# Experts' stage of a two-model kernel: router and token rows taken from unnormalised tiles, expert numbers planned first, last sums inside the loop, output in four pieces

## The chip, the cores and the metric

One Trainium2 chip, one core. The time is device microseconds of one execution; the kernel before has three timed runs. All data and weights are 32-bit floats.

## The reference

The input is 256 tokens of width 1024. A first network of four layers runs, then a second of two layers, whose last part is what the change touches:

```python
h = rmsnorm_2(x, norm_ffn[1])             # x * rsqrt(mean(x*x) + 1e-5) * w
logits = (hf @ w_router)                  # 256 x 8
top_vals, top_idx = lax.top_k(logits, 2)
gates = jax.nn.softmax(top_vals, axis=-1)
# each token goes through its two experts:
expert(xb, e) = (silu(xb @ w_gate[e]) * (xb @ w_up[e])) @ w_down[e]   # 1024 -> 3584 -> 1024
x = x + sum over the two experts of gate * expert(h)
return rmsnorm_2(x, norm_final)
```

The norm divides a whole token by one number, its root mean square, so it changes neither which two logits are largest nor their order. It scales the difference of the two, on which the gates depend.

## The kernel before, in words

The residual stream X lies transposed in SBUF, as eight tiles of 128 channels x 256 tokens. The program is written out by hand for five queues that meet at semaphores: PE (matmuls), DVE, ACT, POOL and SP, which issues the weight loads. The order of work on each is the order of the code; nothing schedules it.

**Into the experts.** `residual` on DVE adds the last product of the second mixer to X two tiles at a time (L1599) and squares them (L1549, summed into S by L1557). `norm` then makes the normalised tiles H: PE sums the squares over channels (`summed`, L600, two records of the profile per call, as for all matmuls here), ACT takes the root (L1177), DVE inverts it and lays it on a diagonal (L1671, L1544), PE spreads it over the partitions (`spread_roots`, L608), and DVE multiplies eight tiles (L1680, H<-X). In other stages, those for which `early` holds, `residual` also writes U = X times the norm's gain (`u_tiles`, L1576), and PE's first product starts from U. `moe` was not one of them.

**Planning.** In `moe` PE multiplies H with the router's weights (L996, 128x8 results), then transposes H into token rows (L1001), which ACT copies to SBUF as `h_tok` (L1472). DVE picks the two best experts of each token (L2181 to L2196, `chosen`). Five small products of PE (L1007 to L1011) give each token's place within its expert and each expert's size. DVE computes the gates, ranks the experts by size, reorders seven facts by rank (L2228, L2232, `passes`), among them the expert's number, and writes the numbers as integers (`plan_i`, L2234). For those SP waits: it reads a number per expert and starts loading that expert's weights, slots of 2 MB into four buffers, a fifth for the last slot (L431). DVE then makes a placement matrix (`put`, L2240), and PE gathers the first expert's tokens with it from `h_tok` (`gather`, L1025), which ACT copies out in two halves (L1479).

**The expert passes.** Seven passes are written out, for experts in falling order of size with 4, 3, 3, 3, 3, 3 and 2 units of 32 tokens, and a loop follows with 2 units for the eighth expert and for tokens that did not fit. The number of loop passes comes from the data. A pass has 14 slots of up and gate weights (PE L1078) and 7 of down weights (L1104). After it ACT copies the result into `y_slot` (L1509), eight pieces for two units, and raises `y_done` once. `scatter` on PE (L1057) multiplies it back to the tokens' columns in four pieces of two tiles, and DVE adds each to X (`add`, L2298). In passes 1 to 6 the scatter of the pass before runs inside the next; that of the last static pass and of the loop passes stands at their end.

**The end.** After the loop DVE squares all of X (L1549), PE sums (L600), root, diagonal and spread follow as above, DVE writes eight tiles H (L1680), and SP stores H with one DMA of 1 MB (L442).

## Time and profile before

| | |
|---|---|
| median of 3 runs | 3094.98 us (3093.48 to 3096.37) |
| the profiled execution | 3095.92 us, its span 3094.1 us |
| PE busy | 2975.9 us (96%) |
| DVE, ACT busy | 1011.7 us (33%), 441.5 us (14%) |
| mean DMA rate | 243 GB/s |
| granted TensorE clock, mean | 0.989 of 2.4 GHz |

A row of the timeline gives start, duration, engine, line, operation and how many instructions it merges, and in brackets how long the engine was idle before and for whom it waited.

### The profile page before, as it was taken

The page shows a single profiled execution, that of the slowest core. Times are in us where ns is not written, and L with a number is a line of the kernel's source. Part 1 is how long each engine was busy: PE and PEld are TensorE (multiplying, and loading weights), DVE is VectorE, ACT ScalarE, POOL GpSimd, SP SyncE. Part 2 cuts the span into 40 slices and gives each one's busy share as a digit, 9 for nine tenths or more (in the row PEclk, how much of TensorE's full clock was granted, in tenths as well). Part 3 has the DMA queues.
Part 4 walks back from the last instruction along what each step waited for, and adds up shares of the span by engine and source line. Part 5 has one row for each costly group of instructions (what it writes and reads, how often), then busy time and mean ns, then how long its engine had stood idle before and what let it go on. Part 6 is the DMA issues. An engine that isn't in the chain of part 4 may idle for free.

```text
span 3094.1 us, 49146 instructions
## 1 busy us (share of the span) xinstructions
PE 2975.9 (96%) x21346; PEld 2233.0 (72%) x21346; DVE 1011.7 (33%) x2300; ACT 441.5 (14%) x902; POOL 92.9 (3%) x180
## 2 busy tenths in 40 slices
PE   5999997999999999999999999998999999999877
PEld 4888886888898888888888888885445345344334
DVE  5526633465354652223327400363100100100101
ACT  1102203221133210102202000121000100100100
POOL 1111000110001100000000000000000000000000
PEclk9999999999999999999999999998999999999998
DMA  9649642685434965444353444434789999999996
GB/s 374 262 176 361 225 162 82 242 319 174 163 109 167 351 214 179 144 142 150 137 166 121 136 151 142 158 108 198 292 321 389 367 382 392 365 382 392 425 421 264
DMA packets 96396, 750.56 MB, mean 243 GB/s; under 512 B 10576, under 2 KB 10960, under 8 KB 46032
## 3 DMA queue, kind: packets, MB, share of 16 engines
q1 hardware_dynamic: 70864, 655.48, 55.8%
q0 software_dynamic: 25344, 92.29, 8.1%
q8 instruction: 153, 2.51, 0.3%
q14 instruction: 35, 0.29, 0.0%
HBM read 746.68 MB, written 1.05 MB: 242 GB/s over the span
## 4 chain that ended last, share of the span: by engine, by line
PE 91%; DMA 5%; DVE 2%; ACT 1%; SPq 1%; issue 0%; DVEq 0%; ACTq 0%
PE ps L487 27%; PE ps L1078 17%; PE ps L564 16%; PE ps L1104 8%; PE ps L652 4%; PE ps L860 3%; PE ps L517 2%; PE ps L497 2%; PE ps L583 2%; PE ps L985 2%; PE ps L783 2%; DMA A<-w_moe_down 1%; PE ps L1057 1%; DMA B<-w_moe_down 1%; DMA B<-w_moe_up 1%; PE ps L1025 1%
## 5 line engine op out<-in xcount | busy, mean ns | idle before, releaser
L487 PE MATMUL ps<-H,ring 128*128 128x256 f32 x3872 | 838.5, 379 | 0.0
L487 PEld LDWEIGHTS ps<-H,ring 128*128 128x128 f32 x3872 | 735.1, 190 | 100.5 <-issue 1.0
L564 PE MATMUL ps<-A,ring 128*128 128x256 f32 x2272 | 491.5, 379 | 0.0
L564 PEld LDWEIGHTS ps<-A,ring 128*128 128x128 f32 x2272 | 431.7, 190 | 58.7
L1078 PE MATMUL ps<-ring,B 128*32 128x512 f32 (+1 forms) x3680 | 325.1, 509 | 11.5 <-DMA ring<-w_moe_up 11.2
L1078 PEld LDWEIGHTS ps<-ring,B 128*32 128x32 f32 x3680 | 121.8, 110 | 209.6 <-issue 157.7
L1078 PE MATMUL ps<-B 128*32 128x512 f32 x2208 | 242.3, 593 | 6.0 <-DMA B<-w_moe_up 6.0
L1800 DVE SCALAR_TENSOR_TENSOR C<-ps,vec,C 128x255 f32<-128x255 f32 (+1 forms) x336 | 146.5, 477 | 202.3 <-ACT C L1242 199.3
L2286 DVE TENSOR_TENSOR C<-C,ps 128x256 f32<-128x256 f32 (+1 forms) x92 | 35.7, 388 | 480.0 <-ACT C L1499 480.0
L1078 PEld LDWEIGHTS ps<-B 128*32 128x32 f32 x2208 | 71.7, 110 | 166.2 <-issue 155.3
L1708 DVE SCALAR_TENSOR_TENSOR B<-B,cact 128x1024 f32<-128x1024 f32 x160 | 188.8, 1220 | 8.6 <-DMA B<-w_ada 8.4
L1104 PE MATMUL ps<-B,A 128*32 128x256 f32 x2944 | 162.7, 379 | 9.5 <-DMA B<-w_moe_down 9.5
L1104 PEld LDWEIGHTS ps<-B,A 128*32 128x32 f32 x2944 | 94.9, 110 | 75.2 <-DMA B<-w_moe_down 13.4
L2298 DVE TENSOR_TENSOR X<-X,ps 128x512 f32<-128x512 f32 x32 | 22.0, 688 | 373.3 <-PE ps L1057 372.7
L860 PE MATMUL ps<-H,ring 128*128 128x256 f32 x640 | 143.8, 380 | 0.0
L1595 DVE SCALAR_TENSOR_TENSOR X<-ps,gcol,X 128x256 f32<-128x256 f32 x64 | 28.7, 480 | 333.1 <-PE ps L564 295.6
L860 PEld LDWEIGHTS ps<-H,ring 128*128 128x128 f32 x640 | 120.2, 190 | 16.8 <-issue 1.2
L1242 ACT ACTIVATE C<-ps,vec 128x256 f32<-128x256 f32 x168 | 85.7, 560 | 292.4 <-PE ps L487 289.8
L652 PE MATMUL ps<-ring,H 128*128 128x256 f32 x512 | 110.8, 379 | 0.0
L652 PEld LDWEIGHTS ps<-ring,H 128*128 128x128 f32 x512 | 97.3, 190 | 13.2
L462 POOL DMA_DIRECT2D B<-w_ada x144 | 75.7, 528 | 901.5 <-PE ps L583 516.3
L1499 ACT ACTIVATE C<-ps 128x256 f32<-128x256 f32 (+1 forms) x92 | 32.9, 358 | 468.9 <-PE ps L1078 468.9
(377 smaller groups left out, 2269.7 us busy)
## 6 DMA issues: line engine op xcount, KB each, us to landing
ring<-w_moe_up SPq DMA_DIRECT2D x64, 2048.0 KB, 10.2
B<-w_moe_up SPq DMA_DIRECT2D x48, 2048.0 KB, 10.3
ring<-w_ff_up SPq DMA_DIRECT2D x88, 1024.0 KB, 8.1
B<-w_ada POOLq DMA_DIRECT2D x144, 512.0 KB, 8.8
B<-w_moe_down SPq DMA_DIRECT2D x32, 2048.0 KB, 10.0
ring<-w_ff_down SPq DMA_DIRECT2D x64, 704.0 KB, 4.0
ring<-w_gm_in SPq DMA_DIRECT2D x32, 1024.0 KB, 5.0
ring<-w_moe_down SPq DMA_DIRECT2D x16, 2048.0 KB, 9.9
```

The lines of the kernel that those rows point to most:

```text
L462: pool.dma_start(buf, ins["w_ada"][ADA_FIRST + q]).then_inc(ready, 16)
L487: last = mm(bank[:, j * n:(j + 1) * n], ring[:, slot, k * 256 + j * P:k * 256 + j * P + P], src[:, k, :], start=(k == 0), stop=(k == KD - 1))
L497: last = mm(bank[:, j * TOK:(j + 1) * TOK], ring[:, slot, k * 256 + j * P:k * 256 + j * P + P], H[:, k, :], start=(k == 0), stop=(k == KD ...
L517: last = mm(bank[:, 0:n], ring[:, g0 % RING, o:o + P], U[:, k, 0:n], start=(k == 0), stop=(k == KD - 1))
L564: last = mm(bank, ring[:, g % RING, k * P:(k + 1) * P], src[:, kk, :], start=(kk == 0), stop=(kk == kt - 1))
L652: last = mm(ps[m % 4][:, t * TOK:(t + 1) * TOK], H[:, k, t * P:(t + 1) * P], ring[:, (g0 + m) % RING, k * 256:(k + 1) * 256], start=(k == ...
L860: last = mm(ps[t % 4][:, j * TOK:(j + 1) * TOK], ring[:, (g0 + t) % RING, o:o + P], H[:, k, :], start=(k == 0), stop=(k == KD - 1))
L1078: last = mm(ps[u][g * UNIT:(g + 1) * UNIT, 0:width], hg[:, k, u * UNIT:(u + 1) * UNIT], slot[:, (4 * i + g) * width:(4 * i + g + 1) * widt ...
L1104: last = mm(ps[4 + u // 2][g * UNIT:(g + 1) * UNIT, (u % 2) * TOK:(u % 2 + 1) * TOK], hidden_t(f, u), slot[:, i * D + g * TOK:i * D + (g + ...
L1242: ins = af(C[:, b % 4, half, :], src[:, half * TOK:(half + 1) * TOK], ACT.Identity, bias=vec[:, bass.ds(c + 3, 1)], scale=vec[:, bass.ds(c ...
L1708: return stt(out=w, in0=w, scalar=1.0, in1=cact[:, :], op0=ALU.mult, op1=ALU.mult, accum_out=mod[:, n:n + 1])
L1800: ins = stt(out=o, in0=src[:, half * TOK:(half + 1) * TOK - d], scalar=vec[:, c + 2 - d:c + 3 - d], in1=o, op0=ALU.mult, op1=ALU.add)
```

## The change

1. **U instead of H.** `residual` now calls `u_tiles` for `moe` too, and for the last tile before the square instead of after it. PE's `moe` starts with the router on U (six tiles, then the seventh, then the eighth, as they come), then the sums of squares, into ps[5]. `norm` of `moe` makes no diagonal, no spread and no H. The token rows are transposed from U, the first token half before the counting products and the second behind them, and ACT multiplies by the inverse root (one number per partition there) as it copies them. The difference of the two best logits is multiplied by the same number on DVE.
2. **Numbers first.** PE makes the sizes before the places. DVE ranks and writes `plan_i` from the one fact that it needs, then the four facts that `put` needs, then `put`; the gates, their exponential on ACT and the two gate facts come behind it.
3. **First expert.** Slots 0 and 1 of the first pass wait for the first half of the gathered tokens only, slot 2 for the second.
4. **Results out by piece.** ACT copies `y_slot` column group by column group and raises `y_done` four times a pass, and each piece of `scatter` waits for its own group.
5. **Last sums in the loop.** In every loop pass DVE squares two tiles of X right after each of the four adds, and PE sums pair m - 1 behind piece m of the scatter; the last pair is summed behind the loop. The squares behind the loop go.
6. **Output** in four DMAs of two tiles each.

```diff
-            h_ready.wait(sp, h_total)
-            sp.dma_start(out, H[:, :, :]).then_inc(out_done, 16)
-            sp.wait_ge(out_done, 16)
+            h_ready.wait(sp, h_total - KD)
+            for m in range(4):
+                h_ready.wait(sp, 2)
+                sp.dma_start(out[:, 2 * m:2 * m + 2, :], H[:, 2 * m:2 * m + 2, :]).then_inc(out_done, 16)
+            sp.wait_ge(out_done, 64)
...
+            def last_sums(m):
+
+                for k in (2 * m, 2 * m + 1):
+                    for t in range(2):
+                        last = mm(ps[5][:, t:t + 1], U[:, k, t * P:(t + 1) * P], mean[:, 0:1],
+                                  start=k + t == 0, stop=k == KD - 1 and t == 1)
+                return last
...
+                if kind == "final_2":
+                    pe.wait_ge(last_squared, ends[0] * 4)
+                    last_sums(3).then_inc(stat_done.sem, 1)
...
             def moe(_):
-                h_ready.wait(pe, KD)
+                for k in range(KD):
+                    if k in (0, 6, 7):
+                        u_ready.wait(pe)
+                    for t in range(2):
+                        last = mm(ps[4][:, t * 8:(t + 1) * 8], U[:, k, t * P:(t + 1) * P],
+                                  V("router", k * EXPERTS, EXPERTS), start=(k + t == 0), stop=(k == KD - 1 and t == 1))
+                last.then_inc(pe_done.sem, 1)
                 banks_back("moe")
...
+                summed(5)
...
-                def scatter(r):
-
-                    pe.wait_ge(y_done, r + 1)
+                def scatter(r, loop=False):
+
                     for m in range(4):
+                        pe.wait_ge(y_done, r * 4 + (m + 1))
...
                         last.then_inc(side_done, 1)
+                        if loop and m:
+                            pe.wait_ge(last_squared, r * 4 + m)
+                            last_sums(m - 1)
...
+                                if not loop and r == 0 and c == 0 and u == 0 and j in (0, 2):
+                                    pe.wait_ge(side_copied, 1 + j // 2)
...
             def moe(_):
+                dve_act.wait(act)
                 pe_done.skip(act, 1)
+                for t in range(2):
+                    pe_done.wait(act, 3 if t else 1)
+                    for n in (2 * t, 2 * t + 1):
+                        ins = af(B[:, 8 + 2 * n:10 + 2 * n, :].rearrange("p a t -> p (a t)"), ps[n][:, :], ACT.Identity,
+                                 scale=small[:, 24 + t:25 + t])
+                ins.then_inc(act_pe.tick(), 1)
                 dve_act.wait(act)
                 af(small[:, 40:42], small[:, 38:40], ACT.Exp).then_inc(act_done.tick(), 1)
...
-                    for u in range(nu):
-                        for g in range(4):
+                    for g in range(4):
+                        for u in range(nu):
...
+                if nxt[0] == "moe":
+                    u_tiles(nxt, 7, 1)
                 square(7, 1).then_inc(sq_ready.tick(), 1)
...
+                def ranked(lo, hi):
+
+                    for n in range(lo, hi):
+                        ins = tt(rows[:, n, :, :], pick8, outer(facts[:, n, :]), ALU.mult)
+                    step(ins)
+                    for n in range(lo, hi):
+                        ins = nc.vector.tensor_reduce(passes[:, n, 0:EXPERTS], rows[:, n, :, :], AX_X, ALU.add)
+                    step(ins)
...
+                ranked(6, 7)
                 nc.vector.tensor_copy(plan_i[:, 0:EXPERTS], passes[:, 6, 0:EXPERTS]).then_inc(plan_ready, 1)
+                pe_done.wait(dve)
+                step(ts(place_no, ps[7][:, 0:16].rearrange("p (t e) -> p t e", t=2), 1.0, None, ALU.subtract))
+                ranked(0, 4)
...
+                        if loop:
+                            dve.wait_ge(side_added, r * 4 + (m + 2))
+                            tt(U[:, 2 * m:2 * m + 2, 0:TOK], X[:, 2 * m:2 * m + 2, :], X[:, 2 * m:2 * m + 2, :], ALU.mult)\
+                                .then_inc(last_squared, 1)
```

How the instructions stand now. **PE, from the last sums of squares to the first gather, before** (vec is the router's weights, con constants, T the chosen experts; a row is a call):

```order
L608 MATMUL ps<-dg,con 128x128 [waits diag_made]
L608 MATMUL ps<-dg,con 128x128
L996 MATMUL ps<-vec,H 128x8 [waits free_dve,free_act,h_ready]
L996 MATMUL ps<-vec,H 128x8 x15
L1001 MATMUL ps<-con,H 128x128 x16
L1007 MATMUL ps<-T,con 128x8 [waits dve_pe]
L1008 MATMUL ps<-T,con 128x8
L1009 MATMUL ps<-T,con 128x8
L1010 MATMUL ps<-T,con 128x8
L1011 MATMUL ps<-T,con 128x8
L1025 MATMUL ps<-B 128x128 [waits put_done,act_pe]
L1025 MATMUL ps<-B 128x128 x15
```

**The same place after the change**, from the router's last call on; ahead of these rows stand its 15 other calls, the first behind `u_ready`, directly behind the mixer's last product:

```order
L1013 MATMUL ps<-vec,U 128x8
L604 MATMUL ps<-con,S 128x1 [waits sq_ready,free_dve,free_act]
L604 MATMUL ps<-con,S 128x1
L604 MATMUL ps<-con,T 128x1 [waits sq_ready]
L604 MATMUL ps<-con,T 128x1
L1022 MATMUL ps<-con,U 128x128 x8
L1030 MATMUL ps<-T,con 128x8 [waits dve_pe]
L1031 MATMUL ps<-T,con 128x8
L1032 MATMUL ps<-T,con 128x8
L1033 MATMUL ps<-T,con 128x8
L1034 MATMUL ps<-T,con 128x8
L1022 MATMUL ps<-con,U 128x128 x8
```

The spread and the wait for H are gone, the sums stand behind the router, and half of the transposes stands behind the counting products.

**DVE, from the facts of the plan to the first placement matrix, before** (rt holds the logits' work, T the facts):

```order
L2219 COPY T<-ps 128x8
L2221 SCALAR_TENSOR_TENSOR T<-T,con 128x8 [waits dve_step]
L2223 TENSOR_TENSOR T<-T 128x64 [waits dve_step]
L2224 TENSOR_REDUCE T<-T 128x8 [waits dve_step]
L2225 TENSOR_TENSOR T<-T,con 128x64 [waits dve_step]
L2228 TENSOR_TENSOR T<-T 128x64 [waits dve_step]
L2228 TENSOR_TENSOR T<-T 128x64 x6
L2229 TENSOR_TENSOR T<-T 128x64
L2232 TENSOR_REDUCE passes<-T 128x8 [waits dve_step]
L2232 TENSOR_REDUCE passes<-T 128x8 x6
L2234 CAST plan_i<-passes 128x8 [waits dve_step]
L2240 TENSOR_SCALAR B<-con,passes 128x128 x2
```

**After**, from the sizes on:

```order
L2261 COPY T<-ps 128x8 [waits pe_done]
L2263 SCALAR_TENSOR_TENSOR T<-T,con 128x8 [waits dve_step]
L2265 TENSOR_TENSOR T<-T 128x64 [waits dve_step]
L2266 TENSOR_REDUCE T<-T 128x8 [waits dve_step]
L2267 TENSOR_TENSOR T<-T,con 128x64 [waits dve_step]
L2254 TENSOR_TENSOR T<-T 128x64 [waits dve_step]
L2257 TENSOR_REDUCE passes<-T 128x8 [waits dve_step]
L2269 CAST plan_i<-passes 128x8 [waits dve_step]
L2271 TENSOR_SCALAR T<-ps 128x16 [waits pe_done]
L2254 TENSOR_TENSOR T<-T 128x64 [waits dve_step]
L2254 TENSOR_TENSOR T<-T 128x64 x3
L2257 TENSOR_REDUCE passes<-T 128x8 [waits dve_step]
```

Of the seven facts one is reordered ahead of `plan_i`, four between it and the placement matrix, and the gates' work (the next rows of DVE) moved behind.

**PE, the end of the loop and what follows it, before and after** (the first rows are the third and fourth piece of the scatter):

```order
L1057 MATMUL ps<-B 128x256 [waits side_added]
L1057 MATMUL ps<-B 128x256
L1054 REGISTER_ALU
L1057 MATMUL ps<-B 128x256 [waits side_added]
L1057 MATMUL ps<-B 128x256
L1125 REGISTER_ALU
L1125 COMPARE_AND_BRANCH
L600 MATMUL ps<-con,T 128x1 [waits sq_ready]
L600 MATMUL ps<-con,T 128x1 x3
L600 MATMUL ps<-con,T 128x1 [waits sq_ready]
L600 MATMUL ps<-con,T 128x1 x3
L600 MATMUL ps<-con,T 128x1 [waits sq_ready]
```

```order
L612 MATMUL ps<-con,U 128x1 [waits last_squared]
L612 MATMUL ps<-con,U 128x1 x3
L1074 REGISTER_ALU
L1081 MATMUL ps<-B 128x256 [waits side_added,y_done]
L1081 MATMUL ps<-B 128x256
L612 MATMUL ps<-con,U 128x1 [waits last_squared]
L612 MATMUL ps<-con,U 128x1 x3
L1156 REGISTER_ALU
L1156 COMPARE_AND_BRANCH
L636 REGISTER_ALU
L612 MATMUL ps<-con,U 128x1 [waits last_squared]
L612 MATMUL ps<-con,U 128x1 x3
```

The sums, 16 calls behind the loop before, stand in four groups of four, three of them inside it.

## Rows read from the trace of the kernel before

**Rows 1.** The page's part 4: the chain that ended last, by engine.
```profile
PE 91%; DMA 5%; DVE 2%; ACT 1%; SPq 1%; issue 0%; DVEq 0%; ACTq 0%
```

**Rows 2.** Timeline, last add to router: start us, us, engine, line, instruction, idle before.
```profile
2100.94 0.42 DVE L1599 TENSOR_TENSOR X<-X,ps 128x256 f32<-128x256 f32 x1 [2.04 <-PE ps L985]
...
2108.03 7.00 PE L996 MATMUL ps<-vec,H 128*128 128x8 f32 x32 [3.32 <-DVE H L1680]
```

**Rows 3.** Timeline, planning on PE and DVE.
```profile
2114.88 3.65 PE L1001 MATMUL ps<-con,H 128*128 128x128 f32 x16
...
2117.62 0.17 DVE L2196 TENSOR_TENSOR T<-rt 128x16 f32<-128x16 f32 x1
...
2120.59 0.16 DVE L2219 COPY T<-ps 128x8 f32<-128x8 f32 x1
...
2121.76 1.04 DVE L2228 TENSOR_TENSOR T<-T 128x64 f32<-128x64 f32 x7
...
2123.85 0.17 DVE L2234 CAST plan_i<-passes 128x8 int32<-128x8 f32 x1
2123.93 0.60 DVE L2240 TENSOR_SCALAR B<-con,passes 128x128 f32<-128x128 f32 x2
```

**Rows 4.** Timeline, first gather and first expert weights.
```profile
2124.67 6.61 PE L1025 MATMUL ps<-B 128*128 128x128 f32 x32 [4.20 <-DVE B L2240]
...
2125.06 0.90 SPq L431 DMA_DIRECT2D ring<-w_moe_up  x2
...
2131.31 0.60 ACT L1479 ACTIVATE B<-ps 128x512 f32<-128x512 f32 x1 [2.26 <-PE ps L1025]
...
2133.23 15.64 PE L1078 MATMUL ps<-ring,B 128*32 128x512 f32 x128 [1.95 <-DMA ring<-w_moe_up]
```

**Rows 5.** Windows there: stretch; busy PE, PEld, DVE, ACT, POOL; PEclk, DMA share, GB/s.
```profile
2102.00:2104.00 2.00, 0.99 (x6) 0.90 (x7) 0.59 (x2) 1.47 (x2) 0.00 (x0) 0.81 0.00 0
...
2110.00:2112.00 2.00, 2.00 (x11) 2.00 (x11) 0.00 (x0) 0.00 (x0) 0.00 (x0) 0.50 0.00 0
...
2130.00:2132.00 2.00, 1.28 (x9) 1.08 (x8) 0.09 (x2) 0.67 (x2) 0.00 (x0) 0.86 0.98 418
...
2134.00:2136.00 2.00, 2.00 (x15) 0.64 (x11) 0.00 (x0) 0.00 (x0) 0.00 (x0) 0.50 1.01 434
```

**Rows 6.** Timeline, the gather of the next pass.
```profile
2203.73 3.81 PE L1025 MATMUL ps<-B 128*128 128x96 f32 x32
```

**Rows 7.** The chain in order of time: start us, us, what.
```profile
2073.28 27.64 PE ps L985 x128
...
2297.99 41.34 PE ps L1078 x384
```

**Rows 8.** Timeline, from the sixth static pass into the loop pass.
```profile
2963.82 3.09 ACT L1509 ACTIVATE B<-ps 32x256 f32<-32x256 f32 x8 [34.43 <-PE ps L1104]
...
2972.64 7.07 PE L1078 MATMUL ps<-ring,B 128*32 128x512 f32 x64 [0.18 <-issue]
```

**Rows 9.** Windows, start of the loop pass.
```profile
2976.00:2980.00 4.00, 4.00 (x44) 1.26 (x40) 0.00 (x0) 0.00 (x0) 0.00 (x0) 1.00 0.87 311
2980.00:2990.00 10.00, 10.00 (x96) 2.92 (x88) 1.53 (x4) 0.77 (x2) 0.00 (x0) 1.00 1.02 434
```

**Rows 10.** Timeline, the end.
```profile
3068.16 3.09 ACT L1509 ACTIVATE B<-ps 32x256 f32<-32x256 f32 x8 [20.62 <-PE ps L1104]
...
3071.37 5.40 PE L1057 MATMUL ps<-B 128*128 128x256 f32 x16 [3.28 <-ACT B L1509]
...
3077.53 2.50 DVE L1549 TENSOR_TENSOR T<-X 128x512 f32<-128x512 f32 x4
...
3078.28 5.95 PE L600 MATMUL ps<-con,T 128*128 128x1 f32 x32 [1.50 <-DVE T L1549]
...
3089.76 0.35 SPq L442 DMA_DIRECT2D out<-H  x1
```

**Rows 11.** The page's part 6, DMA issues.
```profile
out<-H SPq DMA_DIRECT2D x1, 1024.0 KB, 3.9
```

More of the change, by code:

```diff
@@ L352, in hidden_t @@
             return flat_a[:, o:o + n * UNIT]
-        h_total = KD * sum(kind not in ("ada", "final_1") for kind, _ in stages)
+        h_total = KD * sum(kind not in ("ada", "final_1", "moe") for kind, _ in stages)
         block = ctx.enter_context(nc.Block())
@@ L1176, in norm @@
                 stat_done.wait(act)
[L1177 removed]
+                af(small[:, 24:26], ps[5 if kind in ("moe", "final_2") else 6][:, 0:2], ACT.Sqrt, bias=eps[:, 0:1] if shift is not None else eps[:, 1:2])\
                     .then_inc(root_done.tick(), 1)
@@ L2244, in moe @@
                 put(place, 0, units(0), slice(0, 1)).then_inc(put_done, 1)
+                act_done.wait(dve)
+                step(ts(small[:, 42:44], small[:, 40:42], 1.0, None, ALU.add))
+                step(nc.vector.reciprocal(small[:, 42:44], small[:, 42:44]))
+                step(tt(small[:, 44:46], small[:, 40:42], small[:, 42:44], ALU.mult))
+                tt(one, one, each(small[:, 42:44]), ALU.mult)
+                step(tt(two, two, each(small[:, 44:46]), ALU.mult))
+                step(tt(gate, one, two, ALU.add))
+                step(tt(sized8, pick8, outer(size), ALU.mult))
+                ranked(4, 6)
                 nm = len(MORE)
```

88 lines of the change are left out of this document (38 added, 50 removed).

## The prediction

> **What bounds the kernel now.** I read the chain that ended last, then the timeline around the two places that the change touches, then the granted clock there. PE holds 91% of the chain [rows 1], so time comes off only where PE stands still, or works at half its clock, on work that nothing else covers. There are three such places. Between the last add to X, at 2100.94, and the first expert matmul, at 2133.23, lie 32.3 us in which no weights flow until SP issues the first load at 2125.06 [rows 2, 4]. Between the last static pass and the loop pass, ACT copies for 3.1 us with PE idle, and the scatter follows; the loop pass starts at 2972.64 [rows 8]. From the end of the loop pass, at 3068.16, to the end of the span run copies, scatter, squares, sums, norm and one store [rows 10], 25.9 us. The loop ran once, as these rows also show. The six passes with four and three units are PE's own time at full clock, so what they start earlier they end earlier. I write times of the new kernel on the old trace's clock.
>
> **1. Up to the first weights.** The last matmul of the mixer ends as DVE's add starts, at 2100.94. The router can now follow it: six of its tiles of U are written before, the last is ready after one operation of the kind of the add, 0.42 us, which is before PE has got through six tiles. Before, the router waited for sums, root, spread and H until 2108.03 [rows 2]. Its 32 records took 7.00 us at half clock (0.219 us each). Their price at full clock is not in the trace; the nearest row is the next pass's gather, 32 records in 3.81 us (0.119 us each) [rows 6]. In the window 2102 to 2104 the mean clock is 0.81, so it fell at about 2103.2, 2.3 us after the mixer's last matmul [rows 5]. I let it fall there again: 19 records at full clock, 13 at half (2.85 us), router done at 2106.1. The bounds are 2104.7 (all full) and 2107.9 (all half).
>
> From the router's end to the chosen experts DVE took 2117.79 - 2115.03 = 2.76 us [rows 2, 3]; that gives 2108.9. PE meanwhile does the sums (8 records at 5.95/32 = 0.186 us, 1.5 us [rows 10]) and the first eight transposes (half of 3.65 us [rows 3]) and is free at 2109.4: PE, not DVE, is late here by 0.2 us net of its reaction. From the chosen experts to the copy of the sizes went 2.80 us with five products; three of them now come later, and a call of this shape costs 0.44 us (7.00/16), so 1.5 us stay, 0.3 of which was PE's reaction: sizes at 2110.6.
>
> From there to the end of the cast went 3.43 us. Eight multiplies and seven reductions took 2.09 us of it, to the start of the cast [rows 3]; one of each stays, some 0.5 us with the waits between. The cast ends at 2112.45, and SP issues as before 1.04 us later, at 2113.5, 11.6 us earlier than now. The first slot arrived 8.17 us after issue [rows 4]: **2121.7**.
>
> The gather must be done by then too. Behind the cast come four multiplies and four reductions (8/15 of 2.09, 1.1 us), one small operation and the wait (0.3) and `put`, 0.60 us [rows 3]: 2114.5. PE's three other products (1.3 us) and eight transposes (1.8 us) end at 2113.6, and ACT's last two copies, 0.60 us each by [rows 4], at 2114.8. The scaling that they now do adds no instruction; its inverse root is ready before 2110. The gather starts at 2114.9 and takes 6.64 us [rows 4]: 2121.5. Two chains end within 0.2 us of each other, so neither half-measure pays. The split wait of the first slots takes ACT's last copy (0.60 us, [rows 4]) off the path. The first expert matmul starts at 2121.7, **11.5 us** earlier. With the router's bounds it is 9.7 to 13.0. What moved behind, the exponential and the gates, is first needed by pass 0's gate placement, tens of us later, and costs nothing; without that cover it would cost some 3 us.
>
> **2. The clock under the first slots.** The first 128 records of pass 0 took 15.64 us [rows 4]; at 41.34/384 us each [rows 7] they would take 13.8. PE stood idle for 1.95 us before them, and the clock, back by 2132, fell to half again at 2134 [rows 5]. With 0.2 us of idleness it may hold: between 0 and 1.85 us; I take **1.2**, nearer to the upper end, since the gather had brought the clock back before the gap.
>
> **3. Into the loop pass.** The first piece of the scatter can start after two copies instead of eight, 2.3 us earlier, and PE, idle for less, may keep its clock: up to 4.2 us in all. But from here the loads bound: in the loop pass the DMA share is 1.02 at 434 GB/s, and only from 2976 to 2980 is it lower, at 311 [rows 9]. The queue has run dry there because PE has not yet given back a slot. An earlier start fills this hole and nothing more: (434 - 311)/434 x 4 = **1.1 us**; bounds 0 and 4.2.
>
> **4. From the last matmul to the root.** Scatter starts 2.3 us earlier, at 3069.05. PE then has 16 records of scatter (5.40 us) and 32 of sums (5.95 us) [rows 10], now interleaved, without the 1.5 us wait for squares in between, which took 2.50 us for all four on DVE. One piece of DVE's work, an add of 0.69 and a square of 0.63 us, fits under the 1.4 to 1.5 us that PE spends on each piece or group, so PE hardly waits: sums done at 3080.4 instead of 3084.23, 3.8 us. At full clock, a record of scatter at the mixer's 27.64/128 = 0.216 us [rows 7], one of sums at 0.119 [rows 6], PE has 7.3 us of work and waits about 2 us for DVE, before the first sums and the last ones: done at 3078.3, 5.9 us. PE's clock fell and rose in these rows; I take **4.3**, near the end at their own rates. The low end, 3.0, has PE waiting 0.3 us for every square. Squares and sums are added to a loop that runs once, so none is paid twice; each further pass would cost some 6 us.
>
> **5. The store.** Root, spread and H keep their time. The single store was issued at 3089.76 and landed 3.9 us later [rows 10, 11]. The last piece, issued at the same moment, has a quarter of the bytes, and the other three, 0.8 us apart, are ahead of it. At 434 GB/s [rows 9] three quarters of 1 MB are **1.8 us**. The ends are 0.8 (some pieces queue, or short rows of 2 KB cost more) and 2.9 (three quarters of 3.9). The Trainium skill, "DMA: Bandwidth & Descriptors", Anatomy of one DMA, gives a store about 2.0 us fixed plus its bytes at 436 GB/s, for the software path; by that the old store takes 4.4 us, half a us over the row, and the last piece 2.6, a gain of 1.3 instead of 1.8.
>
> **The sum:** 11.5 + 1.2 + 1.1 + 4.3 + 1.8 = 19.9 us. The profiled execution took 3095.92, which gives 3076.0; the median of the runs is 0.9 lower, so I forecast **3075.0 us**. A measurement of this kernel can tell about 0.2%, 6 us, from no change.
>
> **Rivals.**
> *The clock holds.* If unbroken work kept the clock up, router, sums and transposes would run at full rate: weights at about 2119.6 (13.6 us), gather done before them, so that PE idles and part 2 gives nothing, and 5.9 us at the end: 13.6 + 1.1 + 5.9 + 1.8 = 22.4, 3072.6 us. Against it, PE was busy all of 2110 to 2112, and from 2108 to 2120 almost without a gap, at half clock [rows 2, 3, 5]. That tells of coming back, less of staying up. The Trainium skill, "TensorE: Matmul & The Clock Gate", Why this matters for your kernels, has the clock stay up as long as no long gap comes between bursts; by that rule this is the case to expect. Chance 0.15.
> *The gather is late.* If U's half transposes, ACT's scaled copies and their semaphores put the gather 3 us behind the weights, and the sums wait for squares at the end (3.0), then 8.7 + 0 + 1.1 + 3.0 + 1.0 = 13.8, 3081.2 us. For it: four engines hand over six times there. Chance 0.14.
> *The change does not do what it says.* The loads of the first passes could be bound elsewhere, so that the earlier number only makes slots wait. Then the end alone gives 1.1 + 3.0 + 1.0: 3090 us. Against it, PE waited for exactly that load [rows 4]. Chance 0.03.
> *Slower.* Pass 0 starts at half clock, and stays there. A record may then take up to twice its 0.108 us [rows 7], so that 20 us are gone after 185 records; over the first 640 records, 69 us at full clock, it would lose up to 69 us and come to 3145 us. For it: PE now arrives from narrow work, with a stop between the first slots, and the old trace shows half clock there (0.50, 1.2 GHz, [rows 5]). Against it: the 128 records with that stretch in them lost 1.85 us in all, and the clock had come back under the gather just ahead. Chance 0.02.
> The forecast itself: 0.66.
>
> **Range.** All low ends together are 9.7 + 0 + 0 + 3.0 + 0.8 = 13.5, 3081.5; all high ends 13.0 + 1.85 + 1.5 + 5.9 + 2.9, 25.2, 3069.8. I give 3069.0 to 3082.0, which holds the first two rivals and leaves out the last two. Faster by over 0.2%: 0.95; within: 0.03; slower: 0.02.
>
> **What would show it.** Right: router directly behind the mixer, the first load issued 11 to 12 us earlier relative to the last add, PE's idle time before the first expert slot under 0.5 us; no dip in the DMA rate at the start of the loop pass; root 4 us earlier behind the last down matmul; the last store landing in about 2.1 us. Wrong: a clock of 1.00 through the router (first rival), PE waiting for ACT's token rows or for `put` (second), the first load issued earlier but passes 1 to 6 no shorter in distance to it, or half clock beyond the first slot of pass 0.

## The result, and the profile after

The changed kernel takes **3073.76 us** (median of 4 runs, 3072.67 to 3075.08), the kernel before 3094.23 (4 runs beside them). The ratio is 0.9935, with a 95% interval of 0.9923 to 0.9946, so it is faster by 20.5 us, where 19.9 were forecast. The forecast time was 3075.0 us, and 3073.76 lies inside the forecast range of 3069.0 to 3082.0. The profiled execution took 3075.08 us with a span of 3073.2; PE was busy for 2964.6 us (96%), DVE for 1011.3, ACT for 441.6; mean DMA rate 244 GB/s, mean granted clock 0.994.

The chain that ended last, of the page's part 4, answers to [rows 1]: PE's share is the same.
```profile
PE 91%; DMA 5%; DVE 2%; ACT 1%; SPq 0%; issue 0%; DVEq 0%
```
The timeline of the changed kernel from the last add to the first expert matmul answers to [rows 2 to 4] (line numbers are now the changed kernel's).
```profile
2100.82 4.59 PE L1013 MATMUL ps<-vec,U 128*128 128x8 f32 x32
2101.02 0.42 DVE L1632 TENSOR_TENSOR X<-X,ps 128x256 f32<-128x256 f32 x1 [1.29 <-PE ps L1002]
...
2108.00 0.17 DVE L2230 TENSOR_TENSOR T<-rt 128x16 f32<-128x16 f32 x1
...
2109.60 0.17 DVE L2261 COPY T<-ps 128x8 f32<-128x8 f32 x1 [1.01 <-PE ps L1031]
...
2111.29 0.17 DVE L2269 CAST plan_i<-passes 128x8 int32<-128x8 f32 x1
...
2112.50 0.90 SPq L432 DMA_DIRECT2D ring<-w_moe_up  x2
...
2114.00 5.22 PE L1049 MATMUL ps<-B 128*128 128x128 f32 x32 [1.36 <-ACT B L1503]
...
2119.26 0.60 ACT L1513 ACTIVATE B<-ps 128x512 f32<-128x512 f32 x1 [1.19 <-PE ps L1049]
...
2121.27 13.94 PE L1107 MATMUL ps<-ring,B 128*32 128x512 f32 x128 [2.05 <-DMA ring<-w_moe_up]
```
The router follows the mixer without a pause. The first load is issued 11.48 us after the last add instead of 24.12, and the first expert matmul comes 20.25 us after it instead of 32.29: **12.04 us** earlier, where the forecast had 11.5. But PE waits 2.05 us for the load, and the gather's copies are done at 2119.9, well before it. The two chains that the forecast saw within 0.2 us of each other lie 1.4 us apart.

The granted clock in windows of the same stretch answers to [rows 5].
```profile
2102.00:2104.00 2.00, 2.00 (x17) 2.00 (x17) 0.31 (x2) 0.00 (x0) 0.00 (x0) 0.82 0.00 0
...
2110.00:2112.00 2.00, 2.00 (x10) 2.00 (x11) 1.79 (x11) 0.28 (x1) 0.00 (x0) 0.50 0.00 0
...
2116.00:2118.00 2.00, 2.00 (x16) 2.00 (x15) 1.76 (x12) 0.53 (x1) 0.00 (x0) 0.77 0.97 401
2118.00:2120.00 2.00, 1.22 (x11) 1.03 (x10) 1.90 (x24) 0.79 (x3) 0.00 (x0) 1.00 1.05 434
2120.00:2122.00 2.00, 0.73 (x8) 0.29 (x12) 1.90 (x11) 1.16 (x1) 0.00 (x0) 1.00 1.02 434
2122.00:2124.00 2.00, 2.00 (x24) 0.65 (x20) 1.26 (x10) 0.00 (x0) 0.00 (x0) 1.00 0.99 426
```
The clock falls at about 2103.3, with PE busy without a break through the whole window and the one after, and is back at about 2116.9. It then holds through PE's wait, and the first 128 records of pass 0 take 13.94 us instead of 15.64.

Between the last static pass and the loop pass, timeline and windows answer to [rows 8, 9].
```profile
2950.91 3.12 ACT L1543 ACTIVATE B<-ps 32x256 f32<-32x256 f32 x8 [35.36 <-PE ps L1133]
...
2951.72 4.04 PE L1081 MATMUL ps<-B 128*128 128x256 f32 x16 [0.88 <-ACT B L1543]
...
2955.87 6.64 PE L1107 MATMUL ps<-ring,B 128*32 128x512 f32 x60
```
```profile
2956.00:2960.00 4.00, 4.00 (x40) 1.24 (x40) 0.49 (x1) 0.00 (x0) 0.00 (x0) 1.00 1.00 422
2960.00:2964.00 4.00, 4.00 (x40) 1.22 (x36) 0.00 (x0) 0.00 (x0) 0.00 (x0) 1.00 1.02 430
```
The loop pass starts 4.96 us after ACT's first copy instead of 8.82, and the hole in the DMA rate is gone.

The end in the timeline, and the stores in the page's part 6 asked for that stretch, answer to [rows 10, 11].
```profile
3055.24 3.12 ACT L1543 ACTIVATE B<-ps 32x256 f32<-32x256 f32 x8 [21.13 <-PE ps L1133]
3056.12 1.99 PE L1081 MATMUL ps<-B 128*128 128x256 f32 x8 [0.95 <-ACT B L1543]
...
3058.75 1.05 PE L612 MATMUL ps<-con,U 128*128 128x1 f32 x8 [0.64 <-DVE U L2348]
...
3064.04 1.05 PE L612 MATMUL ps<-con,U 128*128 128x1 f32 x8 [0.70 <-DVE U L2348]
3065.13 0.26 ACT L1208 ACTIVATE small<-ps,eps 128x2 f32<-128x2 f32 x1 [5.47 <-PE ps L612]
...
3068.37 2.63 SPq L445 DMA_DIRECT2D out<-H  x4
```
```profile
out<-H SPq DMA_DIRECT2D x4, 256.0 KB, 2.1
```

From these marks the 20.9 us between the two spans (3094.1 and 3073.2, given to 0.1 us) divide as follows. A mark is the start of the row named; "pass end" is ACT's first copy of a pass's result.

| stretch | before | after | gain | forecast |
|---|---|---|---|---|
| start to last add (untouched) | 2100.94 | 2101.02 | -0.08 | 0 |
| last add to first expert matmul | 32.29 | 20.25 | 12.04 | 11.5 |
| from there to the end of static pass 0 | 150.62 | 148.93 | 1.69 | 1.2 |
| static passes 1 to 6 | 679.97 | 680.71 | -0.74 | 0 |
| end of pass 6 to end of loop pass | 104.34 | 104.33 | 0.01 | 1.1 |
| end of loop pass to root | 16.11 | 9.89 | 6.22 | 4.3 |
| root to end of span | 9.83 | 8.07 | 1.76 | 1.8 |

Three questions were open then. What sets the first expert matmul, and why did pass 0 keep its clock in spite of a 2 us wait? Why did an earlier start of the loop pass bring nothing? And why did the end give 1.9 us more than forecast? Two theories stood against each other. **Structure**: each gain is the instructions and waits taken off the chain. **Clock**: a good part is that the new orders meet a higher granted clock by where they put PE's work.

### The profile page after: what moved, and what is told of

Its sections match the earlier page's. It is cut to its first block, busy times and chain, and to the rows that moved or that the text cites. A ratio compares the mean times of both kernels' runs of the same rounds, so it can differ in the third digit from the quotient of the medians.

```text
span 3073.2 us, 49174 instructions
## 1 busy us (share of the span) xinstructions
PE 2964.6 (96%) x21342; PEld 2219.2 (72%) x21342; DVE 1011.3 (33%) x2301; ACT 441.6 (14%) x902; POOL 92.8 (3%) x180
## 4 chain that ended last, share of the span: by engine, by line
PE 91%; DMA 5%; DVE 2%; ACT 1%; SPq 0%; issue 0%; DVEq 0%
PE ps L491 27%; PE ps L1107 16%; PE ps L568 16%; PE ps L1133 8%; PE ps L669 4%; PE ps L877 3%; PE ps L521 2%; PE ps L501 2%; PE ps L587 2%; PE ps L1002 2%; DMA B<-w_moe_up 2%; PE ps L800 2%; DMA B<-w_moe_down 2%; PE ps L1081 1%; PE ps L1049 1%; PE ps L820 1%
## 5 line engine op out<-in xcount | busy, mean ns | idle before, releaser
L1107 PE MATMUL ps<-ring,B 128*32 128x512 f32 (+1 forms) x3680 | 323.4, 507 | 13.7 <-DMA ring<-w_moe_up 13.5
L1133 PE MATMUL ps<-B,A 128*32 128x256 f32 x2944 | 162.7, 379 | 10.6 <-DMA B<-w_moe_down 10.6
## 6 DMA issues: line engine op xcount, KB each, us to landing
B<-w_moe_down SPq DMA_DIRECT2D x32, 2048.0 KB, 10.2
```

The costliest lines, as they stand in the source:

```text
L1107: last = mm(ps[u][g * UNIT:(g + 1) * UNIT, 0:width], hg[:, k, u * UNIT:(u + 1) * UNIT], slot[:, (4 * i + g) * width:(4 * i + g + 1) * widt ...
L1133: last = mm(ps[4 + u // 2][g * UNIT:(g + 1) * UNIT, (u % 2) * TOK:(u % 2 + 1) * TOK], hidden_t(f, u), slot[:, i * D + g * TOK:i * D + (g + ...
```

## The experiments

All times below are medians; "the changed kernel" is the one above. Marks are given from the last add (+20.25 is 20.25 us behind it), since the first 2100 us, whose code is the same in all kernels but for the tiles of U, put that add anywhere from 2098.24 to 2101.52 us in the profiles of this study.

**Controls.** Both kernels again.

> The kernel before, unchanged, for a second profile. Asked of it: the first 128 records of pass 0. If the length of the idle gap before them (1.95 us) decides the clock, they take 15.6 us again, with half clock under them. If it is a matter of where the gap falls, they take anything from 13.8 to 15.7 us. Second question: how much the 104.3 us between the last down matmuls of the last static pass and of the loop pass vary when nothing changes; under 0.3 us if the loads run at a fixed pace.

> The changed kernel, unchanged, for a second profile. The first 128 records of pass 0, 13.94 us in the first profile behind a gap of 2.05 us: again 13.9 if the change removed the cause, up to 15.7 if that was chance. From the last down matmul to the last sum of squares 9.9 us again if the interleaved wide and narrow work holds the clock, up to 11.5 if that was chance too.

> The changed kernel again, timed beside the kernel before and the one with the split first slot on the same chip. Expected: 3073.5 to 3074.5 us, ratio to the kernel before 0.993 to 0.994, every milestone as in its two profiles so far; the cast of the expert numbers 9.2 or 10.4 us after the last add, depending on where the clock falls in the router. Rival (the differences between profiles of the same code are chance from chip to chip of over 1 us): a median outside that range.

Before again: 3093.91 us (one run). The changed kernel again: 3074.45 us (one run), then 3072.17 us (5 runs, 3070.75 to 3073.98; ratio 0.9927, interval 0.9914 to 0.9941). The median of the five lies below what was expected (3073.5 to 3074.5). The first 128 records of pass 0 take 15.58 us in the kernel before, behind a wait of 2.38 us, and 13.94 in both of the changed kernel's, behind 1.91 and 1.71 us: so half clock there comes again with the old front, and not with the length of the wait alone. The distance of the ends of pass 6 and of the loop pass is 104.29 us in the kernel before, 104.34 the first time. From the end of the loop pass to the root it is 9.89 us in both of the changed kernel's.

Two things differ between the profile of the five runs and the first one of the changed kernel. The last add came at 2099.71 instead of 2101.02, and the router kept its clock:
```profile
2099.51 3.63 PE L1013 MATMUL ps<-vec,U 128*128 128x8 f32 x32
...
2108.71 0.17 DVE L2269 CAST plan_i<-passes 128x8 int32<-128x8 f32 x1
```
The same 32 records took 3.63 us here, 4.59 in the first profile; the windows (0.61 from 2104 to 2106) put the clock's fall at 2104.4, 4.9 us after the router's start and 1.3 us behind its end, in the first transposes; in the first profile it fell 2.5 us after the start, inside the router. The cast ends 9.17 us after the last add instead of 10.44: the early cast and the late cast, as they are called below. So one kernel has two outcomes here, 1.3 us apart. In ten profiles with the changed order of numbers (the run with the old order is told below) the late one came three times.

**Front alone and end alone.** The first keeps parts 1 to 3 of the change and takes back 4 to 6; the second the reverse. Of the front's kernel:
```diff
-                    for g in range(4):
-                        for u in range(nu):
+                    for u in range(nu):
+                        for g in range(4):
...
-                        ins.then_inc(y_done, 1)
+                    ins.then_inc(y_done, 4)
...
-                        if loop and m:
-                            pe.wait_ge(last_squared, r * 4 + m)
-                            last_sums(m - 1)
...
+                if fresh and shift is None:
+                    for m in range(4):
+                        square(2 * m).then_inc(sq_ready.tick(), 1)
```
The squares and the single store are put back behind the loop as they were.

> Parts 1 to 3 alone: the start of the experts' stage as changed, scatter, last sums and store as before. Theory (the passes with three and four units carry a gain at the start through to the end, the last two passes run at the pace of their loads): the first expert matmul 12.0 us after the last add earlier than before, 1 to 1.7 us more if the clock holds under the first slots, and all of it at the end: 12.5 to 13.5 us faster than before. Rival (the loads of the last two passes take part of it back): under 10 us faster. From the last down matmul to the end of the span 26 us as before.

> Parts 4 to 6 alone on the kernel before. Theory (from the last static pass on the loads bound, so that the earlier scatter there fills the hole in the DMA rate and no more): the loop pass starts 3.9 us earlier behind the last static pass, but its last down matmul comes 0 to 1.1 us earlier, and the end of the kernel gains 6.2 us up to the root and 1.5 to 2 us at the store: 7.5 to 9 us faster in all. Rival (the earlier scatter counts in full): 11 to 12 us faster.

Front alone: 3082.05 us (5 runs, 3078.20 to 3086.01), ratio 0.9959 (0.9945 to 0.9973), 12.3 us below the 3094.35 of the kernel before beside it. End alone: 3087.07 us (10 runs, 3085.33 to 3090.75), ratio 0.9978 (0.9968 to 0.9988), 7.3 us below. The two add up to 19.6 of the 20.5 us. Both lie just under what was expected of them (12.5 to 13.5 and 7.5 to 9 us).

In the front's profile the first expert matmul stands at +18.81, waits 1.77 us for the load, and the first 128 records take 13.94 us: the clock's gain belongs to the front. Of this gain the loop pass took 2.2 us back (it ended 106.49 us after pass 6, told under term 3 below), while the end, expected at 26 us from the last down matmul to the end of the span as before, took 22.6. The end's profile has +31.80 and 15.64 there, as before, and 9.89 us from loop end to root: that gain belongs to the end. The front's kernel, whose end is the old code, shows how much that code depends on the clock. Its way into the loop pass and its end:
```profile
2948.25 3.09 ACT L1536 ACTIVATE B<-ps 32x256 f32<-32x256 f32 x8 [35.30 <-PE ps L1126]
...
2951.39 6.69 PE L1077 MATMUL ps<-B 128*128 128x256 f32 x16 [3.21 <-ACT B L1536]
...
2958.01 7.07 PE L1100 MATMUL ps<-ring,B 128*32 128x512 f32 x64
...
3057.96 3.96 PE L1077 MATMUL ps<-B 128*128 128x256 f32 x16 [3.28 <-ACT B L1536]
...
3063.43 4.07 PE L602 MATMUL ps<-con,T 128*128 128x1 f32 x32 [1.51 <-DVE T L1575]
```
```profile
2952.00:2956.00 4.00, 4.00 (x11) 3.16 (x10) 1.38 (x2) 0.00 (x0) 0.00 (x0) 0.50 0.98 418
...
2960.00:2964.00 4.00, 4.00 (x40) 1.17 (x36) 0.00 (x0) 0.00 (x0) 0.00 (x0) 1.00 0.59 184
```
The first scatter took 6.69 us at half clock, 5.50 in the kernel before, where the clock came back on the way, and 3.97 in its second profile; the scatter at the end 3.96 here and 5.40 before; the sums 4.07 here and 5.95 before. From loop end to root the old code took 16.11, 14.29 (before again) and 12.79 us (here). That the end gave 6.2 us in the first pair is in part the draw of the old kernel's profile: against these three it is 6.2, 4.4 and 2.9 us. The end-alone kernel's median, 7.3 us below the kernel before, less the store's 1.8, says some 5.5 for it over ten runs.

**The store alone.** The changed kernel with one DMA of 1 MB again.
```diff
-            for m in range(4):
-                h_ready.wait(sp, 2)
-                sp.dma_start(out[:, 2 * m:2 * m + 2, :], H[:, 2 * m:2 * m + 2, :]).then_inc(out_done, 16)
+            sp.dma_start(out, H[:, :, :]).then_inc(out_done, 16)
```

> The changed kernel with its output in one DMA of 1 MB again. From the root's start (the last square root on ACT) to the end of the span: 9.8 us as before the change instead of 8.1. If the last piece landed no sooner for being small (rival), 8.1 again.

3074.96 us. Root to end of the span: 9.74 us, with four pieces 8.07. The difference is 1.7 us, as the trace of the pair above had it. (In two profiles with four pieces it is 7.6: there the four records that spread the roots met full clock and took 0.71 and 0.78 us instead of 1.22.)

**Sums behind the loop again.** Copies by piece stay, squares and sums go back (the last two parts of the diff above).

> The changed kernel with squares and sums behind the loop again, the results still coming out by piece. Theory (work moved under the scatter): from the last down matmul to the root 9.9 us become 9.9 plus the squares and the sums that no longer overlap, about 1.5 + 3.9 - 1.05 less what the scatter gains without them, 13 to 14 us at full clock. Rival (the clock made the difference, since the three profiles of the old code took 12.8, 14.3 and 16.1 us): under 11 us wherever the clock stays up.

3073.68 us, span 3071.8, with the early cast (+9.17). Loop end to root 12.27 us instead of 9.89; its sums, behind the full-clock scatter, ran at half clock:
```profile
3052.41 3.96 PE L1079 MATMUL ps<-B 128*128 128x256 f32 x16 [0.95 <-ACT B L1538]
...
3057.88 5.88 PE L604 MATMUL ps<-con,T 128*128 128x1 f32 x32 [1.51 <-DVE T L1577]
```
Of these 2.4 us, 5.88 - 4.07 = 1.8 are the clock's (4.07 is the front-only kernel's time for the same records at full clock), and some 0.6 are structure. The expectation, 13 to 14 us at full clock, was too high: without the 1.8 it would be 10.5 us. That its total equals the changed kernel's is no sign that the sums' place is worth nothing: it had the early cast, 1.3 us, and an early last add.

**Results out by unit again.** The opposite: copies by unit with one signal, sums in the loop.

> The changed kernel with the results released once a pass again. PE is idle for 3.2 us behind the last matmul of both last passes. Theory (the scatter starts 2.3 us later and, with the longer idle time, the clock may fall under it): loop pass starting 7 to 10 us behind the last static pass instead of 5.0, the root 12 to 15 us behind the last down matmul instead of 9.9. The 104.3 us between the last down matmuls of the two passes: 104.3 if a hole of 1 us in the DMA rate costs nothing (as the profiles of before and after have it), 106 if the clock falls for the whole scatter, as in the front-only kernel, where the hole was 2.3 us.

3080.57 us, some 7 us more. PE stands idle for 3.2 us before each scatter instead of 0.9. On the way into the loop pass the scatter ran at half clock (6.76 us), and the pass ended 106.61 us after pass 6 instead of 104.33. At the end 2.3 us are the later start; the rest is the clock, with the last 16 records of sums at 3.58 us, and root came 13.97 us after the loop end instead of 9.89. Together 2.3 + 4.1 = 6.4 us.

**Numbers as late as before.** Places before sizes on PE, and the four facts ahead of the cast.
```diff
-                pe_done.wait(dve, 2)
+                pe_done.wait(dve, 3)
...
+                ranked(0, 4)
                 ranked(6, 7)
                 nc.vector.tensor_copy(plan_i[:, 0:EXPERTS], passes[:, 6, 0:EXPERTS]).then_inc(plan_ready, 1)
```

> The changed kernel with places before sizes on PE, and the four facts of the placement ranked ahead of the expert numbers on DVE; the gates stay behind. Theory (the chain router, plan, load sets the first expert matmul): the load is issued 1.3 us (three products) plus 1.3 us (four multiplies and reductions) later, 14.1 instead of 11.5 us behind the last add, and the first expert matmul comes as much later, 22.8 instead of 20.2. Rival (the gather sets it): 20.2 to 21 us.

3077.59 us. The router ran at full clock (3.63 us), and still the cast ends at +11.83 and the first expert matmul stands at +21.03. Against the early-cast profiles (+9.17) the numbers are 2.7 us later, the matmul 1.9 to 2.2 us. PE then waited 3.30 us, and the clock's gain was gone:
```profile
2113.22 5.25 PE L1049 MATMUL ps<-B 128*128 128x128 f32 x32 [2.13 <-DVE B L2277]
...
2121.77 13.49 PE L1107 MATMUL ps<-ring,B 128*32 128x512 f32 x108 [3.30 <-DMA ring<-w_moe_up]
```
Its first 128 records took 15.64 us. The expected time of the first expert matmul, +22.8, was reckoned from the late cast. The numbers did come as much later as expected, 2.7 us, but the load landed 8.16 us after its issue instead of 8.6 to 8.9. So part 2 of the change is worth about 2 us plus the 1.7 us of the clock, and the loads, not the gather, set the start: the gather's last copy ended at 2119.1, 2.7 us early even so.

**The split wait undone.** Both copies of the gather before the first slot.
```diff
-                    if r:
-                        pe.wait_ge(side_copied, r * 3 + 1)
+                    pe.wait_ge(side_copied, r * 3 + 1 if r else 2)
```

> Part 3 undone alone: the first slot waits for both copies of the gathered tokens again. Theory (the load sets the first expert matmul; in the changed kernel the gather was done about 2 us before it landed): nothing changes; first expert matmul 19 to 20.3 us after the last add, as in the other kernels with the new front, behind a wait for the DMA, and the time is that of the changed kernel, 3073 to 3075 us. Rival (the forecast's tie of the two chains, so that the split wait takes 0.6 us off the path): the wait is put down to ACT's copy, and the first matmul comes 0.6 us later.

3070.73 us (one run, expected 3073 to 3075): first matmul at +19.03 behind 1.80 us of wait for the DMA, within the other profiles with an early cast (18.80 to 19.15). Part 3 is worth nothing here. The time is the lowest of the study mainly because the last add came at 2098.74.

**The first slot in two halves.** If the load is last by 2 us, PE could start on its first half.
```diff
+                    if n == 0 and isinstance(r, int) and r == 0:
+                        sp.dma_start(slot_of[b][:, 0:SLOT // 2], src[:, 0:SLOT // 2]).then_inc(moe_first, 16)
+                        sp.dma_start(slot_of[b][:, SLOT // 2:SLOT], src[:, SLOT // 2:SLOT]).then_inc(moe_ready[b], 16)
+                        continue
```
PE takes the first k-tile of all units, then waits for the second half.

> The changed kernel with the first slot of pass 0 loaded as two DMAs of 1 MB, of which PE needs only the first to begin. Theory (the landing of the first 2 MB sets the start, and the gather is ready 2 us before it): the first half lands some 2 to 2.4 us earlier, so that the first expert matmul comes at 17.9 to 18.3 us after the last add, where the gather and ACT's first copy now set it, PE's idle time before it is under 0.7 us, and the time is 1.5 to 2 us below that of the changed kernel. Rival 1 (the DMA engines, just started, take the halves side by side, so that the first half lands no earlier): PE still waits for the DMA, first matmul as before, and no gain. Rival 2 (passes 0 onward are bound by the flow of weights, so that an earlier start only makes later slots wait): the first matmul is earlier, but the end of the sixth static pass is no earlier relative to the last add (849 us), and the time is that of the changed kernel.

> The kernel with the split first slot once more, because its first five runs (median 3074.49 us) were not faster than the changed kernel's (3072.17 us), although its first expert matmul came 2 us earlier. Theory A (the gain is real, the first five runs drew the later of the two places of the clock's fall in the router and half clock in the last sums): pooled with the first five the ratio to the kernel before comes to 0.992 to 0.9925, and a profile with the cast 9.2 us after the last add has its first expert matmul at 16.9 us after it. Theory B (the gain is given back elsewhere): first matmul again about 2 us earlier, but the ratio to the kernel before stays at 0.993, as in the changed kernel, and some later milestone (end of the sixth static pass, or the root behind the loop) is later by what was won.

3074.49 us (5 runs, 3071.43 to 3074.84; ratio 0.9931, 0.9917 to 0.9944), then 3073.29 us (5 runs, 3071.51 to 3074.03; 0.9932, 0.9918 to 0.9945). No gain over the changed kernel can be measured. Yet the edit did what it was for. In the second profile, with the early cast:
```profile
2112.20 5.61 PE L1054 MATMUL ps<-B 128*128 128x128 f32 x32 [1.36 <-ACT B L1523]
...
2117.74 7.07 PE L1109 MATMUL ps<-ring,B 128*32 128x512 f32 x64
```
The first expert matmul follows the gather with no idle time, at +17.26 (+18.13 with the late cast; 18.80 and 20.11 to 20.25 in the changed kernel's). Of the 1.5 us with the early cast 1.4 are still there at the end of the loop pass: +951.01 against +952.44. They go at the very end, where the code is that of the changed kernel:
```profile
3051.49 3.13 ACT L1563 ACTIVATE B<-ps 32x256 f32<-32x256 f32 x8 [18.46 <-PE ps L1153]
...
3059.21 3.58 PE L617 MATMUL ps<-con,U 128*128 128x1 f32 x16
...
3062.82 0.26 ACT L1228 ACTIVATE small<-ps,eps 128x2 f32<-128x2 f32 x1 [6.90 <-PE ps L617]
```
The window 3058 to 3060 has a mean clock of 0.51 there; in the changed kernel the clock was full until 3065.8, 10.6 us after the loop end. Root comes 11.33 us after the loop end (10.58 in the first profile), where all seven profiles with this end and the whole first slot have 9.89 or 9.90. So theory B of the expectation holds for the second profile, with the clock at the end as the place; in the first the end takes back 0.7 us of the 1.5 to 1.8 that were left at the end of the loop pass. Whether the earlier fall follows from the edit or two profiles drew it by chance isn't settled: nothing near the end was changed.

## Why the prediction was right, and where it was not

**Term 1, up to the first weights (11.5, measured 12.04).** The mechanism is as forecast, and so is most of its working: router 4.59 us against 2.85 + 19 x 0.119 = 5.1 forecast, clock falling about 2.3 us after the mixer's last matmul as in [rows 5], cast at 2111.3 to 2111.5 against 2112.45. That the fall came where the forecast put it was the draw of this profile: in seven of ten the router ran at full clock throughout, and with the first slot whole these have the first expert matmul at +18.80 to +19.15, 12.7 to 13.1 us earlier than the old front's two other profiles (+31.80, +31.88), which is the forecast's upper bound of 13.0. What did not come true is the sentence that two chains end within 0.2 us of each other. The loads were issued 1.0 us earlier than forecast but landed 8.77 us after their issue instead of 8.17 [rows 4], and the gather took 5.22 us instead of 6.64, since the clock came back inside it at 2116.9. The half-measures differ after all: undoing the early numbers costs about 2 us at this point and 1.7 more behind it, undoing the split wait nothing. The sign "PE's idle time before the first expert slot under 0.5 us" was not seen: it is 2.05 us.

**Term 2, the clock under the first slots (1.2, measured 1.7).** The size was near, the reason was wrong. The forecast let the clock hold because PE would stop for only 0.2 us. PE stopped for 2.05 us, no less than before, and it held. What differs lies ahead of the stop: before, PE had waited 4.20 us for the placement matrix and the clock came back late in the gather (0.86 in the window 2130 to 2132 [rows 5]); now the wait there is 1.36 us and the clock is full from 2116.9, 4.4 us before pass 0. That this is the cause is argued, not shown. Every profile with a wait of 1.36 us before the gather kept the clock, every one with 4.2 us lost it. But the run with late numbers, which lost it too, has both waits longer, 2.13 and 3.30 us, and its clock was back 2.2 us before the gather's end, as in the changed kernel; there the second wait may have been enough.

**Term 3, into the loop pass (1.1, measured 0.01).** This term failed. The hole was filled, as forecast, but the loop pass ended 104.3 us after pass 6 in both kernels and in every other profile but two. The forecast took the mean rate for the limit. (It gave this term bounds of 0 and 4.2, but added only 1.5 in its sum of high ends; the result bears on neither.) The last load of the pass was issued 80.0 us (before) and 79.5 us (after) behind the end of pass 6, and the matmuls that waited for it started at the same distance, 100.6 us. How the flow ended differs. Before and after, in the two aligned windows from 8.16 us ahead of the loop end on:
```profile
3060.00:3062.00 2.00, 2.00 (x44) 1.23 (x40) 0.00 (x0) 0.00 (x0) 0.00 (x0) 1.00 0.77 328
3062.00:3064.00 2.00, 1.16 (x24) 0.42 (x16) 0.00 (x0) 0.00 (x0) 0.00 (x0) 1.00 0.25 98
```
```profile
3047.08:3049.08 2.00, 2.00 (x44) 1.23 (x40) 0.00 (x0) 0.00 (x0) 0.00 (x0) 1.00 0.46 197
3049.08:3051.08 2.00, 1.17 (x24) 0.43 (x16) 0.00 (x0) 0.00 (x0) 0.00 (x0) 1.00 0.11 41
```
After the change the DMA share is down to 0.46 where it was 0.77: the flow thins out sooner, and yet the last slot comes no sooner. PE's waits for earlier slots tell when the gain went. Here, before, after, and for the kernel before again, are one wait for an up slot and the first wait behind the pass's gather:
```profile
3024.43 3.66 PE L1078 MATMUL ps<-ring,B 128*32 128x256 f32 x64 [1.32 <-DMA ring<-w_moe_up]
...
3054.61 3.66 PE L1104 MATMUL ps<-B,A 128*32 128x256 f32 x64 [0.50 <-DMA B<-w_moe_down]
```
```profile
3010.87 3.66 PE L1107 MATMUL ps<-ring,B 128*32 128x256 f32 x64 [1.33 <-DMA ring<-w_moe_up]
...
3041.71 3.66 PE L1133 MATMUL ps<-B,A 128*32 128x256 f32 x64 [1.02 <-DMA B<-w_moe_down]
```
```profile
3023.66 3.66 PE L1078 MATMUL ps<-ring,B 128*32 128x256 f32 x64 [1.32 <-DMA ring<-w_moe_up]
...
3054.44 3.66 PE L1104 MATMUL ps<-B,A 128*32 128x256 f32 x64 [0.89 <-DMA B<-w_moe_down]
```
From the end of pass 6 the first of these starts at 60.61, 59.96 and 59.96 us (that end is at 2963.70 in the third), the second at 90.79, 90.80 and 90.74. So the changed kernel did win 0.65 us in the first pair, for most of the pass, and lost it again before the last three slots. In the second profile of the kernel before there was nothing to win, as its 59.96 shows, though the DMA rate dips there too (348 GB/s for 4 us): its scatter ran at full clock. Why the last slots land at the same distance in each is not shown; the DMA share is a mean over the engines. What is shown is the limit of it: where the scatter ran wholly at half clock (front alone, and results by unit), the hole was deeper, 184 and 156 GB/s for 4 us, and the pass ended 106.49 and 106.61 us after pass 6. Part 4 of the change is worth 0 to 2.2 us here, by the clock that it meets.

**Term 4, from the loop's end to the root (4.3, measured 6.22).** The bounds of 3.0 and 5.9 were stated for an old end that takes 16.1 us, and the new one at full clock was worked out as root about 10.2 us after the loop end; it takes 9.89, with waits for DVE of 0.64 and 0.70 us at the two places named. The measured 6.22 lies above both. The mis-sized step is "I take 4.3, near the end at their own rates": in seven profiles of seven with the whole first slot the clock stayed full until the last sums were through. The new end starts PE's work after 0.9 us of idleness instead of 3.3. The old end met half clock to a varying degree, and so did the two half-measures (results by unit, sums behind the loop) and, with the new end's own code, the two profiles with the split first slot.

**Term 5, the store (1.8, measured 1.76).** Right, and the last pieces land 2.1 us after issue, as forecast. By the Trainium skill, "DMA: Bandwidth & Descriptors", Anatomy of one DMA, a store takes 2.0 us plus its bytes at 436 GB/s, on the software path; that is an estimate of 4.4 us for the old store and 2.6 for the last piece, each half a us over its row (3.9 and 2.1), so it too gives a gain of 1.8. The forecast's 1.3 beside it came from taking the Trainium skill's 2.6 from the row's 3.9.

**What wasn't in the sum.** Passes 1 to 6 lost 0.74 us. Five of them take 116.62 us instead of 116.56 in all kernels that keep four waits in the scatter, 0.3 us in all; the rest lies in pass 6, which takes 97.2 to 98.2 us from profile to profile.

**The rivals.** *The clock holds* fell for the front: the windows show 0.50 (1.2 GHz) from 2104 to 2116 with PE busy for 2.00 of 2.00 us in most of them. Part of its sign, a clock of 1.00 through the router, was seen in seven of ten profiles, but there the clock fell in the transposes behind it. The rule of the Trainium skill, "TensorE: Matmul & The Clock Gate", Why this matters for your kernels, asks for no longer idle gaps of PE if the clock is to stay up. It doesn't cover this stretch: the clock fell inside the router, which is 128x8 work, or in the transposes behind it, with no gap at all. At the end the rival's number, 5.9, was the nearer. *The gather is late*, *the change doesn't do what it says* and *slower* did not occur; pass 0 ran at full clock from its first record.

The sum came out 0.6 us from the measured difference because errors of both signs offset each other, which is luck: 0.5 + 0.5 + 1.9 too little in terms 1, 2 and 4, and 1.1 + 0.7 too much in term 3 and in what was left out, 1.0 us net in the two spans. Nor are the terms fixed sizes: with other profiles of the same two kernels term 1 comes to 13.1 and term 4 to 4.4.

Of the two theories, structure has the larger share. Of the 20.9 us the clock has at least 5.0: 1.7 under pass 0, and 3.3 at the end, which is the 6.2 of the pair less the 2.9 that the new end gains on the old one where that ran at full clock.

## What to carry to other kernels

Price a stretch of narrow PE work at both clocks, and look at how long PE stood idle ahead of it and ahead of the work before it: here the same code took 12.8 to 16.1 us, and with shorter waits upstream pass 0 met another clock. A dip in the mean DMA rate is not time lost until the landing of the last load moves. Before taking a gain of 1 us for real, subtract what the untouched part of the program does between profiles, here 3.3 us, by measuring from a mark behind it.

## What the hardware showed that was not expected

- The clock fell during unbroken PE work, and not at a fixed place: in two profiles of the same kernel 2.5 us after the router's start (at 2103.3, inside it) and 4.9 us after (at 2104.4, in the transposes behind it), which moves the cast by 1.3 us.
- It stayed at full through PE's wait of 2.05 us before pass 0, and was lost in the kernel where waits of 2.13 and 3.30 us enclosed the gather, and in the kernel before behind waits of 1.95 and 2.38 us.
- The first 2 MB slot, loaded into idle DMA engines, lands 8.2 to 8.9 us after issue; the rate takes three windows of 2 us to build up (115, 254, 401 GB/s from 2112 on).
- The first half of that slot, as a DMA of its own, was there 6.7 us after its issue at the latest, when PE began on it (the profile with the late cast).
